# Pairs for the key and retention slabs, rotation shifts on ScalarE, and a new order of modulation slabs, in a two-layer trunk step

## The reference, cut to what matters

```python
h = _rmsnorm(xl, norm_mix[l]) * (1.0 + ml[1]) + ml[0]
aq, ak, av, bq, bk, bv, cq, ck, cv, cg, gates = _split_projection(h, w_in[l])   # ck * C_DK ** -0.5
aq = _axial_rope(aq, n_lat)            # x * cos + rot(x) * sin
ak = _axial_rope(ak, n_lat)
a_o = _diff_output(_diff_attention(aq, k_all, v_all, lam), diff_norm[l], lam_init)
b_o = _neighbourhood_attention(bq, bk, bv, cache_b_k[:, l], cache_b_v[:, l], na_rpb[l])
c_raw, _, _ = _bidirectional_retention(cq, ck, cv, log_gamma, state_c_fwd[:, l], state_c_bwd[:, l])
xl = xl + ml[2] * _merge(gates, a_o, b_o, c_o, w_proj_a[l], w_proj_b[l], w_proj_c[l], w_out[l])
xl = xl + ml[5] * _expert_choice_ffn(h, w_router[l], w_exp_gate[l], w_exp_up[l], w_exp_down[l])
```

## Time and profile before

| | us |
|---|---|
| median of 3 runs | 1900.98 |
| lowest and highest | 1900.81, 1901.68 |
| the profiled execution's own time | 1900.78 |
| its span in the profile | 1899.0 |
| PE busy | 1777.8 (94%) |
| DVE busy | 651.9 (34%) |
| ACT busy | 376.9 (20%) |
| POOL busy | 330.0 (17%) |

### The profile page before, as it was taken

One profiled execution on the slowest core, in us unless ns is written; L12 is line 12 of the kernel. 1 busy time (PEld: TensorE's weight loads), 2 busy tenths in 40 slices (PEclk: granted clock), 3 DMA queues, 4 the chain that ended last, 5 costly groups with the idle time before them and its releaser, 6 DMA issues.

```text
span 1899.0 us, 22343 instructions
## 1 busy us (share of the span) xinstructions
PE 1777.8 (94%) x9262; PEld 1053.6 (55%) x9262; DVE 651.9 (34%) x1328; ACT 376.9 (20%) x853; POOL 330.0 (17%) x193
## 2 busy tenths in 40 slices
PE   6999999999999988788799999999999998888887
PEld 3595567999634333233266755689995343333323
DVE  2853354565411211111158433435643111121103
ACT  3223334101301010010132242340112110101002
POOL 2520006953100000000035100276610000000000
PEclk9999999999999999999999999999999999999999
DMA  9525152425999999999992244214378999999996
GB/s 386 202 92 223 66 221 80 178 89 211 363 419 427 428 427 428 428 428 428 405 392 100 89 183 177 100 45 177 134 293 342 428 428 428 427 428 426 428 429 269
DMA packets 55717, 553.19 MB, mean 291 GB/s; under 512 B 6080, under 2 KB 10560, under 8 KB 13632
## 3 DMA queue, kind: packets, MB, share of 16 engines
q1 hardware_dynamic: 51840, 549.13, 70.0%
q10 hardware_dynamic: 3776, 2.62, 0.4%
HBM read 547.54 MB, written 4.19 MB: 291 GB/s over the span
## 4 chain that ended last, share of the span: by engine, by line
PE 67%; DMA 30%; DVE 2%; issue 1%; SPq 0%; ACT 0%; DVEq 0%
PE psum L1403 17%; PE psum L1644 14%; DMA ring<-in_w_up 9%; DMA dense<-in_w_down 8%; PE psum L1152 8%; DMA ring<-in_w_gate 8%; PE psum L1154 7%; DMA dense<-in_w_gate 4%; PE psum L1161 4%; PE psum L471 2%; PE psum L1322 2%; PE psum L1111 2%; PE psum L1242 1%; PE psum L1606 1%; PE psum L1498 1%; DMA ring<-in_w_in 1%
## 5 line engine op out<-in xcount | busy, mean ns | idle before, releaser
L1644 PE MATMUL psum<-ring,dense 128*64 128x512 f32 x992 | 223.5, 595 | 34.0 <-DMA ring<-in_w_gate 19.0
L1644 PE MATMUL psum<-dense 128*64 128x512 f32 x704 | 159.2, 596 | 22.6 <-DMA dense<-in_w_gate 16.8
L1644 PEld LDWEIGHTS psum<-ring,dense 128*64 128x64 f32 x992 | 71.0, 137 | 177.3 <-issue 144.5
L1152 PE MATMUL psum<-hT,ring 128*128 128x384 f32 x464 | 153.4, 488 | 0.0
L2513 DVE TENSOR_TENSOR state<-state,psum 128x512 f32<-128x512 f32 x32 | 22.0, 689 | 369.7 <-PE psum L1644 331.7
L888 POOL TENSOR_TENSOR tmp<-square 128x384 f32<-128x384 f32 x5 | 5.0, 997 | 817.8 <-ACT square L1780 817.8
L1154 PE MATMUL psum<-ring,hT 128*128 128x512 f32 x288 | 126.5, 594 | 0.0
L1152 PEld LDWEIGHTS psum<-hT,ring 128*128 128x128 f32 x464 | 87.5, 190 | 60.8 <-issue 1.4
L1644 PEld LDWEIGHTS psum<-dense 128*64 128x64 f32 x704 | 50.5, 137 | 125.6 <-issue 92.2
L2088 ACT ACTIVATE kcT<-psum 32x512 f32<-32x512 f32 x60 | 35.2, 587 | 421.0 <-PE psum L1644 420.6
L2550 DVE COPY decays<-psum 16x512 f32<-16x512 f32 x60 | 41.3, 689 | 218.1 <-PE psum L1644 217.7
(11 more groups left out here) (329 smaller groups left out, 2725.1 us busy)
## 6 DMA issues: line engine op xcount, KB each, us to landing
ring<-in_w_in SPq DMA_DIRECT2D x60, 1024.0 KB, 10.4
dense<-in_w_gate SPq DMA_DIRECT2D x30, 2048.0 KB, 36.8
ring<-in_w_up SPq DMA_DIRECT2D x30, 2048.0 KB, 37.4
ring<-in_w_gate SPq DMA_DIRECT2D x30, 2048.0 KB, 36.4
wide<-in_w_up SPq DMA_DIRECT2D x22, 2048.0 KB, 37.9
dense<-in_w_down SPq DMA_DIRECT2D x20, 2048.0 KB, 40.3
ring<-in_w_mod SPq DMA_DIRECT2D x38, 1024.0 KB, 8.6
ring<-in_w_down SPq DMA_DIRECT2D x18, 2048.0 KB, 39.3
```

Source lines behind the costliest of these rows:

```text
L1152: last = M.matmul(psum[:, bank, 0:T], ring[:, n % RING, k, cols], hT[:, k, :], start=k == 0, stop=k == KD - 1)
L1644: last = M.matmul(psum[HALF * half:HALF * (half + 1), bank, :], lhsT(k), SPARE_BLOCKS[2 * kk + half] if spare else w[:, kk, half * SLAB:(h ...
```

## The change

- Slabs 1 and 6 are computed as pairs too (`PAIRED`), which makes 8 pairs in each layer. The two pairs of the keys come in the front (`PAIRS_AHEAD`), after slab 0 and the first value group; the other six fill steps 0 to 11 of loop A. The weight sums of the last pair lie in the constants' place. CK is no longer scaled while it is copied, but by two ScalarE operations in loop B.
- The sine table is permuted. ScalarE copies the four 32-row quarters of a chunk to their shifted places (`halves_swapped`), and VectorE does one 128x256 product with the sine in place of four 32x256 ones (`rotate`).
- `decays()` and `decay_logs()` come first in the front on their engines, ahead of the rotation and ahead of the copy of group 0.
- The window is added to the bias in eight operations in place of two, with weight sums between.
- In loop B some groups are cut in two (`begun`, `rest`); in layer 0 the modulation slabs `m[2:5]` lie ahead of slab 8 in `SLABS`, in layer 1 `m[2:4]`. Steps 12 and 13 of loop B are left without a filler.
- `finish_mods(layer, 4, 9)` moves from ahead of the first decayed attention of the retention to its third head.

```diff
-FIRST_PAIRED, LAST_PAIRED = 3, 4
-Z_PAIRS = [(slab, p) for slab in (FIRST_PAIRED, LAST_PAIRED) for p in range(2)]
+PAIRED = {1: 12, 3: 4, 4: 16, 6: 20}
+Z_PAIRS = [(slab, p) for slab in PAIRED for p in range(2)]
+PAIRS_AHEAD = 2
...
-    put("sin", np.sin(ang) * np.where(np.arange(P) % 64 < 32, 1.0, -1.0)[:, None])
+    put("sin", (np.sin(ang) * np.where(np.arange(P) % 64 < 32, 1.0, -1.0)[:, None])[np.arange(P) ^ 32])
...
-            a, b, c = [Z_PAIR_BANKS[(i + n) % 3] for n in range(3)]
+            banks = S + TR[1:] if i < PAIRS_AHEAD else Z_PAIR_BANKS
+            a, b, c = [banks[(i + n) % 3] for n in range(3)]
...
-        MODS_IN_A = 3
+        MODS_IN_A = 2
...
-            return [[("pair", l, i), ("half", l, i)][h:h + 1] for i in range(len(Z_PAIRS)) for h in range(2)] + [[("z", l, 19 + t)] for t in range(3)] + [
-                [("mod", l, m[0]), ("mod", l, m[1])], [("modT", l, m[0]), ("mod", l, m[2])], [("modT", l, m[1]), ("modT", l, m[2])]]
+            steps = [[("pair", l, i), ("half", l, i)][h:h + 1] for i in range(PAIRS_AHEAD, len(Z_PAIRS)) for h in range(2)]
+            return steps + [[("mod", l, m[0]), ("mod", l, m[1])], [("modT", l, m[0]), ("modT", l, m[1]), ("z", l, 19)]]
...
-            steps = [[("norm", l, t), ("z", l, 22 + t)] for t in range(4)] + [[("z", l, 26)], [("z", l, 27)]]
-            steps += [[("z", l, 28), ("mod", l, m[3]), ("mod", l, m[4])], [("z", l, 29)], [("z", l, 30)], [("modT", l, m[3]), ("mod", l, m[5])],
-                      [("z", l, 31)], [("z", l, 32)]]
+            steps = [[("norm", l, 0), ("z", l, 20)], [("norm", l, 1), ("z", l, 21)], [("norm", l, 2), ("z", l, 26)], [("norm", l, 3), ("begun", l, 27)],
+                     [("rest", l, 27), ("mod", l, m[2])], [("modT", l, m[2]), ("begun", l, 28)], [("rest", l, 28), ("mod", l, m[3])],
+                     [("modT", l, m[3]), ("z", l, 29)], [("mod", l, m[4]), ("begun", l, 30)], [("rest", l, 30), ("modT", l, m[4]), ("mod", l, m[5])],
+                     [("modT", l, m[5]), ("z", l, 31)]]
...
-                return steps + [[("modT", l, m[4]), ("mod", l, m[6])], [("modT", l, m[5]), ("modT", l, m[6])]]
-            return steps + [[("modT", l, m[4])], [("modT", l, m[5])]]
+                return steps[0:4] + [[("rest", l, 27), ("begun", l, 28)], [("rest", l, 28), ("mod", l, m[2])],
+                                     [("modT", l, m[2]), ("mod", l, m[3]), ("mod", l, m[4])], [("modT", l, m[3]), ("modT", l, m[4]), ("z", l, 29)],
+                                     [("mod", l, m[5]), ("begun", l, 30)], [("rest", l, 30), ("modT", l, m[5]), ("mod", l, m[6])],
+                                     [("modT", l, m[6]), ("z", l, 31)], [("z", l, 32)], [], []]
+            return steps + [[("z", l, 32)], [], []]
...
-        SLABS = [FIRST_SLABS[l] + [("w_in", j) for j in range(1, 6)] + [("mod", j) for j in DENSE_MODS[l][0:MODS_IN_A]]
-                 + [("w_in", 6), ("w_in", 7), ("mod", DENSE_MODS[l][3]), ("mod", DENSE_MODS[l][4]), ("w_in", 8)] + [("mod", j) for j in DENSE_MODS[l][5:]]
+        LATER_MODS = [5 if len(m) == 7 else 4 for m in DENSE_MODS]
+        SLABS = [FIRST_SLABS[l] + [("w_in", j) for j in (2, 1, 3, 4, 6)] + [("mod", j) for j in DENSE_MODS[l][0:MODS_IN_A]]
+                 + [("w_in", 5), ("w_in", 7)] + [("mod", j) for j in DENSE_MODS[l][2:LATER_MODS[l]]] + [("w_in", 8)]
+                 + [("mod", j) for j in DENSE_MODS[l][LATER_MODS[l]:]]
...
-                        sums = Z_WEIGHT_SUMS[p]
+                        sums = Z_WEIGHT_SUMS[i]
...
+                    def add_window(b):
+                        for part in range(4):
+                            rows = bias[b].rearrange("p h (r c) -> p (h r) c", c=GRID_W)[:, 8 * part:8 * (part + 1)]
+                            G.tensor_tensor(rows, rows, c_("window").unsqueeze(1).to_broadcast([P, 8, GRID_W]), ALU.add).then_inc(bias_ready, 1)
...
+                    pool.wait_ge(bias_in, at(bias_in, 32))
+                    add_window(0)
...
-                    pool.wait_ge(bias_in, at(bias_in, 32))
-                    for b in bias:
-                        rows = b.rearrange("p h (r c) -> p (h r) c", c=GRID_W)
-                        G.tensor_tensor(rows, rows, c_("window").unsqueeze(1).to_broadcast([P, 32, GRID_W]), ALU.add).then_inc(bias_ready, 1)
...
+                    add_window(1)
+                    for i in range(4, len(Z_PAIRS) - 1):
+                        z_pair_weight_sums(i)
+                    pool.wait_ge(bias_ready, at(bias_ready, 8))
+                    pool.wait_ge(chunk_ready, at(chunk_ready, 1))
+                    pool.wait_ge(lam_sum, at(lam_sum, 1))
+                    z_pair_weight_sums(len(Z_PAIRS) - 1)
...
-                    def z_group(l, g):
+                    def z_begun(l, g):
+                        z_group(l, g, range(KD // 2))
+                    def z_rest(l, g):
+                        z_group(l, g, range(KD // 2, KD))
+                    def z_group(l, g, chunks=range(KD)):
...
+                            pe.wait_ge(z_read, f_of("z", l, 0))
+                        elif i == PAIRS_AHEAD:
...
-                        else:
+                        if i >= 1:
...
-                    for g in range(Z_FIRST):
+                    def halves_swapped(c):
+                        if c < 4:
+                            sc.wait_ge(z_read, f_of("z", layer, c) + 1)
+                        else:
+                            sc.wait_ge(z_pair_summed, at(z_pair_summed, 4 * (c // 2 - 1)))
+                        if c >= 2:
+                            sc.wait_ge(rope_done, at(rope_done, c - 1))
+                        for q in range(4):
+                            quadrant, other = slice(32 * q, 32 * q + 32), slice(32 * (q ^ 1), 32 * (q ^ 1) + 32)
+                            A_.activation(tmp[other, c % 2, 0:2 * P], zT[quadrant, ROTATED[c], LAT], ACT.Copy).then_inc(rope_part, 1)
+                    decay_logs()
+                    for g in Z_AHEAD[0:4]:
...
-                        if g == 4:
-                            decay_logs()
-                        if g == 5:
-                            decay_inside()
-                        if g == 6:
-                            decay_across()
+                        halves_swapped(g)
+                    decay_inside()
+                    read_z(layer, Z_AHEAD[4])
+                    copy_z_first(layer, 0)
+                    decay_across()
+                    halves_swapped(4)
+                    halves_swapped(5)
+                    copy_z_first(layer, 1)
+                    halves_swapped(6)
+                    halves_swapped(7)
+                    for g in Z_AHEAD[5:]:
+                        read_z(layer, g)
...
+                    sc.wait_ge(z_pair_summed, at(z_pair_summed, 4 * PAIRS_AHEAD))
...
+                        if t in (5, 6):
+                            sc.wait_ge(z_pair_summed, at(z_pair_summed, 4 * len(Z_PAIRS)))
+                            A_.activation(zT[:, CK + t - 5, :], zT[:, CK + t - 5, :], ACT.Copy, scale=SCALE).then_inc(ck_scaled, 1)
...
-                    for c in range(8):
-                        if c == 2:
-                            decays()
-                        dve.wait_ge(z_read, f_of("z", layer, c) + 1)
-                        if c >= 2:
-                            dve.wait_ge(rope_done, at(rope_done, c - 1))
-                        for q in range(4):
-                            quadrant, other = slice(32 * q, 32 * q + 32), slice(32 * (q ^ 1), 32 * (q ^ 1) + 32)
-                            V.tensor_tensor(tmp[other, c % 2, 0:2 * P], zT[quadrant, ROTATED[c], LAT], c_("sin")[quadrant], ALU.mult).then_inc(rope_part, 1)
+                    def rotate(c):
...
+                        V.tensor_tensor(tmp[:, c % 2, 0:2 * P], tmp[:, c % 2, 0:2 * P], c_("sin"), ALU.mult)
...
+                    decays()
+                    for c in range(4):
+                        rotate(c)
+                    for i in range(PAIRS_AHEAD):
+                        z_begin_sums(i)
+                        z_end_sums(i)
+                        dve.wait_ge(z_pair_summed, at(z_pair_summed, 4 * i + 4))
+                        rotate(4 + 2 * i)
+                        rotate(5 + 2 * i)
...
-                        if n < 2 * len(Z_PAIRS):
-                            (z_begin_sums, z_end_sums)[n % 2](n // 2)
+                        (z_begin_sums, z_end_sums)[n % 2](PAIRS_AHEAD + n // 2)
...
-                    finish_mods(layer, 4, 9)
-                    finish_scale(layer, scale_ffn_all, slice(32, 40), slice(56, 64)).then_inc(mod2_ready, 1)
-                    dve.wait_ge(mod2_ready, at(mod2_ready, 1))
...
+                        if m == 2:
+                            finish_mods(layer, 4, 9)
+                            finish_scale(layer, scale_ffn_all, slice(32, 40), slice(56, 64)).then_inc(mod2_ready, 1)
+                            dve.wait_ge(mod2_ready, at(mod2_ready, 1))
```

(11 more changed lines are left out.)

50 lines of the change are left out of this document (29 added, 21 removed).

## The result

The changed kernel took 1904.63 us (median of 20 runs, 1900.55 to 1909.33 us), the kernel before 1901.38 us (20 runs, 1900.21 to 1903.52 us). The ratio is 1.0017, with an interval of 1.0011 to 1.0022: slower, though by less than the 0.2% that was called a tie ahead of the run. The forecast was 1897.4 us with a range to 1901.5 us, so the time lies outside it by 3.1 us. The profiled execution took 1904.28 us with a span of 1902.4 us, 3.5 us and 3.4 us more than before.

The account below looks back on a forecast made before the run. The PE was taken to set the time in fronts and loops. Fronts of +1.1 and +1.3 us and loops of -2.9 us per layer sum to -3.4 us: 1900.78 us becomes 1897.4 us, range 1890.0 to 1901.5 us.

Parts of the forecast that it names:

- The pairs: Slabs 1 and 6: two pairs take 18.20 us against 20.64 us direct, saving 4.88 us in each layer.
- The rival of the narrow matmuls: Slabs computed as pairs: weight loads stand between matmuls, so halved width saves nothing; 1924 us, chance 0.01.
- The mechanism of the stall: Fronts: late scalars and GpSimd's token sums block `decays` operations one by one, delaying logarithms, group 0's copy and group 2.
- between two sums: Fronts: if the last two operations of `decays` slipped between two token sums, the stall would be 2 us less per layer.
- The stall is 3.8 us in layer 0 and 4.1 us in layer 1: Fronts: PE idle time before group 2, which can start at 49.1 us and 979.0 us, not 45.3 and 974.9 us.
- The other moved pieces are neutral: Loops: modulation slabs and value groups swap at equal length; steps 0 to 11 keep at least 3.4 us of filler.
- The rotation in time: Layer 0's front: rotation ends at 89.5 us, PE reaches the scores at 93.0 us; 3.5 us cover, no cost.
- slower, by the rotation: Fronts: ScalarE's shifts or contended VectorE operations exceed their bounds and the 3.5 us cover; 1905.4 us, chance 0.06.
- Norm and `finish_mods`: Norm after loop A: +0.45 us behind a group's copy; `finish_mods` off the decayed attention's way: -0.7 us; each layer.
- The loops as a sum: Loops and retention: slab 6, fewer filler starts, the norm and `finish_mods` sum to -2.9 us in each layer.
- the forecast's own rival: Fronts without stall, as `decays` operations get between sums or scalars land sooner: 1889.5 us, chance 0.12.
- the gain is eaten: Both layers: a further 1.5 to 5 us of small waits at norms, pairs or thinner loop B steps; 1899 to 1902.5 us, chance 0.22.

Follow-up runs that it names:

- experiment 5: Changed kernel with the decay logarithms behind the copies of groups 0 and 1, and group 29 between the transposes in layer 0's step 7: 1893.34 us, ratio 0.9956.
- Experiments 1: Changed kernel, but ScalarE copies groups 0 and 1 before the decay logarithms, and group 2 before the shifts: 1897.21 us, ratio 0.9978.
- 3: Changed kernel, but GpSimd holds its first token sum back until the maximum of `decays` is through: 1899.06 us, ratio 0.9987.
- experiment 2: Changed kernel, but in step 7 of layer 0's loop B group 29 stands between the two transposes, not behind both: 1902.27 us, ratio 1.0003.
- experiment 4: Changed kernel with 14 unused matmuls on constants ahead of group 2 in layer 1's front, to keep the PE busy: 1902.89 us, ratio 1.0011.
- experiment 6: On top of experiment 5, group 19 ahead of the two transposes in step 13 of loop A: 1893.12 us, ratio 0.9959.
- 8: The changed kernel run and profiled once more, without an edit: 1903.36 us, ratio 1.0013.

## Why the prediction was wrong

**What bounds the kernel** held. A microsecond taken from the PE in fronts and loops came out at the end: experiment 5 begins the decayed attention of layer 1 at 1213.2 us in place of 1221.3 us, 8.1 us sooner, and its span is 7.5 us shorter (1891.5 us against 1899.0 us).

**The pairs** held to the hundredth: two pairs stand in the chain with 18.20 us in both fronts, and records of half the width cost half. The rival of the narrow matmuls is out. (Its time was added up wrongly: 1897.4 us and four times 9.1 us are some 1934 us; the 1924 us take the savings off a second time.)

**The mechanism of the stall** held: late scalars, sums in a row, small operations blocked one by one. Experiments 1 and 3 show it. **Its price** was mis-sized in two ways that partly cancelled. The text had 3.8 us and 4.1 us of idle time; the traces have 1.66 to 1.81 us or 3.47 us in layer 0, and 3.47 to 3.67 us in layer 1. The case "between two sums" was in the prediction as 2 us less, but thought of as small operations that slip between sums; what happened in the two short cases is that the front and its sums began later (41.46 us in place of 40.45 us in the profile of the change), the scalars landed at about the same time, and every blocked operation ended one sum sooner. What the text did not have at all is the time after the idle time: 1.7 us in layer 1, because the next groups ran at the lower clock. The step "The stall is 3.8 us in layer 0 and 4.1 us in layer 1" thus failed in its size, as it counted an idle PE as idle time alone. Idle and slow time together were 6.8 us in the profile of the change (1.66 + 3.47 + 1.7), under the 7.9 us of the forecast, so this error did not make the kernel slower than forecast there; that the two parts nearly made up for each other is luck. In experiment 2 they were some 11 us (3.47 + 2.7 + 3.54 + 1.6). The Trainium skill (TensorE: Matmul & The Clock Gate, "What's actually happening") has two levels and an array that falls back to the lower one when it stands idle; by that rule, the trace agrees for layer 1, though experiment 4 ran at the full level behind 3.47 us of idle time.

**"The other moved pieces are neutral"** is the step that failed in kind, and it is the larger one: 2.4 us of wait in step 7 of layer 0, in every trace that has the old order, and 1.5 to 1.7 us of slow clock behind it in four of the five. Experiments 1 and 5, which differ by this order alone, are 3.9 us apart, more than the 3.1 us by which the time missed the range; experiment 2, whose front still stalled, won back 2.4 us by its median. The prediction asked that each step had at least 3.4 us of filler. The length was there; what it left out is the order inside a step. A group behind two short transposes needs the first of them read, and that read stands behind the step's softmax on ScalarE. The filler was long enough to hide the softmax and was itself waiting for it. Experiment 2 moves one piece, and the wait is gone.

**The rotation in time** held: its last operation ended at 88.5 us (forecast 89.5 us), the PE was through at 92.2 us, and in place of the old wait there is the copy of group 10, 0.61 us and 0.24 us of signals. The shifts took 0.415 us each (at most 0.49 us was assumed), the contended operations of the last two chunks 1.37 to 1.49 us, over the 1.27 us that were assumed. The rival "slower, by the rotation" did not happen: the kernel was slower for other reasons.

**Norm and `finish_mods`** held as waits: the norm waited 0.68 us where it had waited up to 0.28 us (forecast +0.45 us), and `finish_mods` gave 0.9 us each (forecast 0.7 us). But experiment 6 took the norm's extra wait away and gained 0.1 us. **The loops as a sum** came out at -2.0 us in layer 1 where -2.9 us was forecast, and in 5 also at -2.1 us in layer 0 (195.97 us before, 193.85 us now). No experiment takes the missing 0.8 to 0.9 us in each layer apart, but the trace of the change has two waits in each layer that the kernel before does not have. In layer 1:

```profile
1105.95 3.64 PE L1136 MATMUL psum<-ring,silu_c 128*32 128x512 f32 x32 [0.35 <-DVE dense L2324]
...
1193.17 1.92 PE L1136 MATMUL psum<-ring,silu_c 128*32 128x512 f32 x16 [0.23 <-ACT mod_columns L1857]
```

The first modulation slab of loop A waits for VectorE's last addition of the last pair, and one in loop B for a read by ScalarE. They are 0.58 us, of which the forecast had 0.15 us; the rest of the gap stays open.

**The sum again,** by the stretches of the ledger above, measured against forecast: a later start (+1.0 us, forecast 0), the front of layer 0 (-0.7, +1.1), the rest of layer 0 to the decayed attention (+2.1, -2.9), the experts (-0.4, 0), the front of layer 1 (+2.7, +1.3), its loops (-2.0, -2.9) and the rest (+0.7, 0). The differences are +1.0, -1.8, +5.0, -0.4, +1.4, +0.9 and +0.7 us, 6.8 us, which is the way from -3.4 to +3.4 us in the span. The +5.0 us are step 7 with 2.4 and some 1.7 us and the gap of the loops with 0.8 us. The -1.8 us are the shorter stall (-2.1 us), and the +1.4 us the slow clock (+1.7 us) less 0.6 us of stall; 0.3 us is left in each. The +0.7 us behind the loops of layer 1 stay open. The start lies ahead of the changed operations, and it varies among traces of the changed kernels: four matmul records on `square` at 17 us took 2.5 us in some (this one and 5), 2.1 to 2.3 us in others (1, 3 and 8) and 1.6 us in the rest, as in the one trace of the kernel before. With one trace of that kernel it can't be said that the start is as variable there. Where the stall is away, as in 5, the forecast's own rival gave 1889.5 us, and 1893.3 us was measured: 1.1 us of later start, 0.9 us more in the front of layer 0, of which 0.5 us is a wait for a pair's sums, and 1.7 us in the loops.

The rival "the gain is eaten" had the right kind (a thinner step of loop B) but looked at VectorE's late answer and capped the price at 1902.5 us. Of the signs that the prediction named, the idle time of 3.5 to 4.5 us was nearly there in layer 1 (3.47 us) and not in layer 0, where the first copy (47.4 us) also came ahead of the fourth sum's end (48.7 us); the loops were 2.2 us shorter in neither layer.

## What to carry to other kernels

A filler hides a wait only if it doesn't need that wait's result: check for each filler which buffer it writes, who must have read it, and what that reader has in front of it in its own queue. Put the short pieces behind the long one. Price a stall of a few microseconds on TensorE with what may come behind it too: a slow group, 1.5 to 2.7 us here. And a chain of small VectorE operations beside a row of GpSimd operations costs up to one GpSimd operation each; either run it before them or put nothing urgent behind it. Here two edits of order (experiment 5) turned a loss of 3 us into a gain of 8.0 us without a change to what is computed.

## What the runs showed of the hardware that was not expected

- The lower clock after idle time is not certain. After 3.5 to 3.7 us idle in layer 1 all three traces with this wait and no filling matmuls (the changed kernel twice, and 2) had two groups in 12.2 to 12.3 us in place of 10.6 us. After 3.47 us in layer 0 one trace had 8.17 us for a group (2) and one 5.43 us (4); after 1.66 us and 1.81 us there both had 5.43 us. After 2.4 us in step 7 four traces had 6.93 to 7.09 us (the changed kernel, 1, 3 and 4) and one 5.40 us (8). What decides it was not settled.
- The runs of a kernel with these stalls lie further apart: 8.8 us between the fastest and the slowest of 20 runs of the changed kernel and 5.8 to 7.3 us over the 11 of 2, 4 and 8, against 3.3 us over the 20 of the kernel before and 3.4 us and 2.3 us over the 11 of 1 and 3, which are without the long waits in the fronts. That the stalls are the reason is argued, not shown: of the five runs of 6, which has none of them, one took 4.5 us more than the median.
